# Modulation vectors of the second attention layer: VectorE row products in place of TensorE products on a three-slot weight ring

## The reference

```python
def modulation(cond, w_ada, b_ada):
    m = jax.nn.silu(cond) @ w_ada + b_ada
    return [t[..., None, :] for t in jnp.split(m, 6, axis=-1)]

def modulate(h, shift, scale):
    return h * (1 + scale) + shift
...
    for i in range(DEPTH_2):
...
        sh1, sc1, g1, sh2, sc2, g2 = modulation(c, w_ada[i], b_ada[i])
        csh1, csc1, cg1, csh2, csc2, cg2 = modulation(c_ctx, w_ada[i], b_ada[i])

        h = modulate(rms_norm(x, norm1_g[i]), sh1, sc1)
...
        x = x + g1 * (jnp.concatenate([out_a, out_b, out_c], axis=-1) @ w_out[i])
        x = x + g2 * conv_ffn(modulate(rms_norm(x, norm2_g[i]), sh2, sc2),
                              w_up[i], conv_w[i], conv_b[i], w_down[i])
```

## Time and profile before

| what | value |
|---|---|
| median of 3 runs | 1830.97 us (1829.68 to 1835.06) |
| span of the profiled execution | 1832.5 us |
| own time of the profiled execution | not given beside its span |
| PE busy | 1754.7 us, 96% |
| PE weight loads busy | 1573.7 us, 86% |
| DVE busy | 1031.8 us, 56% |
| ACT busy | 863.4 us, 47% |
| POOL busy | 358.7 us, 20% |
| moved by DMA | 258.76 MB, mean 141 GB/s |

### The profile page before, as it was taken

How to read it: one execution, slowest core, us unless ns; L and a number is a source line. 1 busy time by engine, 2 the same in 40 slices (tenths; PEclk the granted TensorE clock), 3 DMA queues, 4 the chain that set the end, 5 groups by cost and what they waited for, 6 DMA issues and landing times.

```text
span 1832.5 us, 30035 instructions
## 1 busy us (share of the span) xinstructions
PE 1754.7 (96%) x12614; PEld 1573.7 (86%) x12614; DVE 1031.8 (56%) x1804; ACT 863.4 (47%) x1292; POOL 358.7 (20%) x220
## 2 busy tenths in 40 slices
PE   6999989999999999999999999999999898899999
PEld 6999878898999999998867878777888787699999
DVE  2477469687676885267754175413552278538840
ACT  4432546447445665445754254313332355546653
POOL 5301540000000115700001301232114200041147
PEclk9999989999999999999989999999999899889999
DMA  6644445444465554421100422154223222025544
GB/s 262 230 185 163 183 158 205 189 181 178 194 259 205 190 186 143 169 99 47 70 1 12 163 81 98 70 194 177 92 83 126 85 92 75 19 102 198 184 150 150
DMA packets 40967, 258.76 MB, mean 141 GB/s; under 512 B 4352, under 2 KB 7552, under 8 KB 14464
## 3 DMA queue, kind: packets, MB, share of 16 engines
q1 hardware_dynamic: 40832, 256.84, 38.2%
HBM read 255.77 MB, written 1.05 MB: 140 GB/s over the span
## 4 chain that ended last, share of the span: by engine, by line
PE 87%; DVE 9%; ACT 3%; issue 1%; POOL 1%; DMA 0%; SPq 0%; DVEq 0%; ACTq 0%
PE acc_psum L194 24%; PE acc_psum L196 23%; PE acc_psum L195 23%; PE acc_psum L2254 3%; PE acc_psum L235 2%; PE acc_psum L2207 2%; PE acc_psum L319 2%; PE acc_psum L2233 2%; PE acc_psum L923 2%; DVE w_low_sb L160 1%; PE acc_psum L254 1%; DVE norm_rt_sb L1575 1%; POOL w_low_sb L160 1%; DVE norm_sq_sb L579 1%; PE acc_psum L353 0%
## 5 line engine op out<-in xcount | busy, mean ns | idle before, releaser
L194 PE MATMUL acc_psum<-h_high_sb,w_high_sb 128*128 128x256 f32 (+1 forms) x2144 | 666.3, 311 | 10.4 <-DVE h_low_sb L386 4.4
L196 PE MATMUL acc_psum<-h_high_sb,w_low_sb 128*128 128x256 f32 (+1 forms) x2144 | 657.5, 307 | 0.0
L195 PE MATMUL acc_psum<-h_low_sb,w_high_sb 128*128 128x256 f32 (+1 forms) x2144 | 657.4, 307 | 0.0
L149 ACT ACTIVATE w_high_sb<-ring_sb 128x1024 fp32r<-128x1024 f32 (+2 forms) x412 | 386.6, 987 | 455.9 <-PE acc_psum L196 262.1
L194 PEld LDWEIGHTS acc_psum<-h_high_sb,w_high_sb 128*128 128x128 f32 x2144 | 411.0, 192 | 41.6 <-issue 18.2
L160 POOL TENSOR_TENSOR w_low_sb<-ring_sb,w_high_sb 128x1024 fp32r<-128x1024 f32 (+2 forms) x150 | 297.6, 2008 | 687.9 <-ACT w_high_sb L149 687.9
L195 PEld LDWEIGHTS acc_psum<-h_low_sb,w_high_sb 128*128 128x128 f32 x2144 | 410.8, 192 | 19.3 <-issue 0.5
L196 PEld LDWEIGHTS acc_psum<-h_high_sb,w_low_sb 128*128 128x128 f32 x2144 | 410.1, 191 | 19.0
L160 DVE TENSOR_TENSOR w_low_sb<-ring_sb,w_high_sb 128x1024 fp32r<-128x1024 f32 (+1 forms) x262 | 306.5, 1211 | 54.8 <-ACT w_high_sb L149 45.4
L1796 DVE SCALAR_TENSOR_TENSOR u_filtered<-acc_psum,par_sb,u_filtered 128x255 f32<-128x255 f32 (+2 forms) x264 | 150.9, 572 | 151.3 <-ACT u_filtered L1903 139.1
L1931 POOL TENSOR_TENSOR u_low<-u_filtered,u_high 128x256 fp32r<-128x256 f32 (+1 forms) x66 | 61.0, 925 | 779.6 <-ACT u_high L1924 779.6
(11 more groups left out here) (296 smaller groups left out, 2043.4 us busy)
## 6 DMA issues: line engine op xcount, KB each, us to landing
ring_sb<-in_w_in SPq DMA_DIRECT2D x68, 1024.0 KB, 6.4
ring_sb<-in_w_up SPq DMA_DIRECT2D x66, 1024.0 KB, 4.8
ring_sb<-in_w_ada SPq DMA_DIRECT2D x48, 1024.0 KB, 4.8
ring_sb<-in_w_down SPq DMA_DIRECT2D x48, 704.0 KB, 4.1
ring_sb<-in_w_out SPq DMA_DIRECT2D x12, 1024.0 KB, 5.1
ring_sb<-in_w_br_hg SPq DMA_DIRECT2D x4, 1024.0 KB, 6.9
ring_sb<-in_w_br_ml SPq DMA_DIRECT2D x4, 1024.0 KB, 7.0
ring_sb<-in_w_br_mb SPq DMA_DIRECT2D x4, 1024.0 KB, 8.0
```

The lines of the kernel that those rows point to most:

```text
L149: self.nc.scalar.activation(self.high[:, g % 2, piece], self.ring[:, c % RING, piece], ACT.Copy)\
L194: nc.tensor.matmul(out, sh, mh, start=start, stop=False)
L195: nc.tensor.matmul(out, sh, ml, start=False, stop=False)
L196: return nc.tensor.matmul(out, sl, mh, start=False, stop=stop)
```

## The change

The 24 units of layer 1's `w_ada` leave the hybrid block and PE. They are laid out by rows of the transposed matrix: a unit is 128 x 2 rows of 1024, so that partition p holds two whole rows. Both condition vectors are laid out whole in each partition (`cond_rows`, 1 MB), loaded at the beginning of `out_projection`, and passed through Silu by ACT. For each unit DVE multiplies each of the two rows by each of the two vectors and sums along the row in the same instruction, with the bias as the start of the sum: four instructions, which write the result's column straight away. The products themselves are not used: two go to `mod_products`, two into the ring's slot. The units ride in attention layer 0 alone: behind units 1 to 3 of the output projection, 4, 6 and 8 of the first `up`, all eight of the first `down`, 2, 4, 6 and 8 of the second `up`, and 0 to 5 of the second `down`. The gains of layer 1's norms are computed behind unit 6 of the second `down` instead of unit 1.

```diff
+ROW_RIDES = {"out": (1, 2, 3), "up0": (4, 6, 8), "down0": tuple(range(DT)), "up1": (2, 4, 6, 8), "down1": tuple(range(6))}
...
+class RowModulation:
...
+    def dot(self, dve, n, c):
+
+        core, slot = self.core, self.core.ring[:, c % RING, :].rearrange("p (j k) -> p j k", j=2)
+        core.wait_loaded(dve, c)
+        if n == 0:
+
+            dve.wait_ge(*self.rows_ready.at(1))
+        else:
+
+            dve.wait_ge(self.multiplied.handle, n)
+        for s in range(2):
+            for j in range(2):
+                t, row = 2 * n + j, slot[:, j, :]
+                ins = core.nc.vector.tensor_tensor_reduce(row if s else self.products[:, j, :], row, self.rows[:, s, :], 1.0,
+                                                          self.bias[:, t, 0:1], ALU.mult, ALU.add, self.result[:, t, s:s + 1])
+        ins.then_inc(*self.multiplied.one())
...
@@ out_projection, SP
+            if side:
+
+                for handle, value in first_use[0]:
+                    sp.wait_ge(handle, value)
+                sp.dma_start(side.rows[:, :, :].rearrange("p a b -> p (a b)"), a["cond_rows"]).then_inc(*side.rows_in.dma())
             core.release(sp, g0 + units, side)
@@ out_projection, PE
-                if side:
-                    if n >= 1:
-                        side.reduce(pe, n - 1, m0 + n - 1)
-                    side.multiply(pe, n, core.place(g0 + n) + 1)
                 behind.pe(pe, n)
             behind.pe(pe, units)
-            if side:
-                side.reduce(pe, units - 1, m0 + units - 1)
             norm.spread(pe)
@@ out_projection, ACT
                 core.split_high(act, g0 + n + 1)
+                if side and n == 0:
+
+                    act.wait_ge(side.rows_in.handle, 16)
+                    core.nc.scalar.activation(side.rows[:, :, :], side.rows[:, :, :], ACT.Silu).then_inc(*side.rows_ready.one())
                 behind.act(act, n)
@@ out_projection, DVE
-                if side:
-                    side.copy(dve, n)
+                if n in rides:
+                    side.dot(dve, m0 + rides.index(n), core.place(g0 + n) + 1)
             norm.reciprocal(dve)
-            if side:
-                side.read(dve, units, m0, units)
@@ down, PE
-                if n in rides:
-                    if rides.index(n) >= 1:
-                        side.reduce(pe, rides.index(n) - 1, m0 + rides.index(n) - 1)
-                    side.multiply(pe, rides.index(n), core.place(g0 + n) + 1)
@@ down, DVE
                     residual(t, bank(t)).then_inc(*free.one())
                 if n in rides:
-                    side.copy(dve, rides.index(n))
+                    side.dot(dve, m0 + rides.index(n), core.place(g0 + n) + 1)
@@ AttentionAhead, DVE
+        if n == (1 if self.i == 0 else 6):
             gains = core.mod_gains
+            if self.rows:
+
+                dve.wait_ge(*self.rows.multiplied.at(6))
```

More of the change, by code:

```diff
@@ L81 @@
 BANKS = 3
+RIDES = tuple(range(1, 2 * (N_ADA * P // UNIT), 2))
+ROW_RIDES = {"out": (1, 2, 3), "up0": (4, 6, 8), "down0": tuple(range(DT)), "up1": (2, 4, 6, 8), "down1": tuple(range(6))}
+assert sum(len(v) for v in ROW_RIDES.values()) == N_ADA * P // UNIT
 class Core:
@@ L679, in modulation_slot @@
             layer = 0 if counts[0] < NM else 1
-            stream.append((a["w_ada_2"][NM * layer + counts[layer]], None))
+            stream.append(((a["w_ada_2"], a["w_ada_rows"])[layer][counts[layer]], None))
             counts[layer] += 1
@@ L704, in build @@
                 for half in range(2):
[L705 to L706 removed]
+                    add("w_up_2", range(up0 + FFH * half, up0 + FFH * (half + 1)), "dve", "pool", ROW_RIDES[f"up{half}"])
+                    add("w_down_2", range(down0 + half, down0 + 2 * DT, 2), "pool", "dve", ROW_RIDES[f"down{half}"])
             else:
@@ L775, in residual @@
                     return f
-                side = None if last else mods[1]
+                side = None if last else rows
                 with arena(f"arena_attention{i}"):
@@ L780, in build @@
                                              [written.at(n) for n in (-3, -2)])
[L781 to L784, removed]
-                out_projection(core, H, T, *joined, residual(2), norm2, core.eps[:, 0:1], side)
@@ L875, in conv_at @@
         return sum(1 for i in range(n) if PLACES[i][0] in ("ml_qk", "xbc"))
-    rides = list(range(1, UNITS, 2))
     NM = N_ADA * P // UNIT
-    first_read = sig("mod_first_read")
     GROUPS, GW = 4, W8 // 4
@@ L1481, in _ @@
             act.wait_ge(par_ready.handle, 16)
-            nc.scalar.activation(mods[0].cond[:, :, 0:2], pv("cond", DT), ACT.Silu).then_inc(*cond_ready.one())
+            nc.scalar.activation(mod.cond[:, :, 0:2], pv("cond", DT), ACT.Silu).then_inc(*cond_ready.one())
             for n in range(UNITS + 1):
@@ L1639, in _ @@
                 if n == 2 * NM + 1:
-                    mods[0].read(dve, NM, 0, NM).then_inc(*first_read.one())
+                    mod.read(dve, NM, 0, NM)
                 if n == 4:
@@ L1692, in _, with out_projection @@
             norm2.reciprocal(dve)
-            mods[1].read(dve, len(rides), 0, len(rides) - NM)
     core.taken = UNITS
-    mods[0].taken, mods[1].taken = NM, len(rides) - NM
-def out_projection(core, H, T, operand, order, banks, first_use, residual, norm, eps, side):
+def out_projection(core, a, H, T, operand, order, banks, first_use, residual, norm, eps, side):
     nc, units = core.nc, 4
@@ L1704, in out_projection @@
     core.taken += units
-    m0 = 0
+    rides = ROW_RIDES["out"] if side else ()
     if side:
         m0 = side.taken
-        side.taken += units
+        side.taken += len(rides)
     behind = NormBehind(norm, free, {n: n for n in range(units)})
@@ L1805, in feed_forward @@
             down(core, (uh, ul), T, seg == 1, down_banks, first_use, residual, hooks[p], side,
-                 () if not side else (1, 3) if p else tuple(range(DT)))
+                 ROW_RIDES[f"down{p}"] if side else ())
             written = core.sig("proj_bank_free")
@@ L1810, in feed_forward, with up @@
             done_before = core.sig("proj_acc_ready")
-def up(core, H, T, first, n_units, lead_tap, conv3, tmp, uh, ul, norm, banks, first_use, done_before):
+def up(core, H, T, first, n_units, lead_tap, conv3, tmp, uh, ul, norm, banks, first_use, done_before, side=None, rides=()):
     nc, psum = core.nc, core.psum
+    if side:
+        m0 = side.taken
+        side.taken += len(rides)
     acc, free = core.sig("up_acc_ready"), core.sig("up_bank_free")
```

85 lines of the change are left out of this document (47 added, 38 removed).

## The result

The changed kernel takes 1860.75 us (median of 4 runs, 1857.5 to 1864.58) beside 1832.58 us for the kernel before in the same sitting (1829.68 to 1835.06): a ratio of 1.015, 95% interval 1.0129 to 1.0171. It is 28.2 us slower, where the prediction had 28. In the two profiled executions, 1855.7 against 1832.5, the difference is 23.2 us.

A forecast was written before the change was run, and what follows sets the result against it. PE, busy 96% of the span, was taken as the bound. Hybrid block -13.4, `down` +13.8 and +11.2, output projection +1.3 gave +12.9; with 15 for port and clock, +28: 1830.97 + 28 = 1859 us, range 1836 to 1884.

The forecast's parts named there:

- The rides taken away, -30.5 us: Units of w_ada leaving PE: 13.4 us in the hybrid block's tail, 3.7 output projection, 10.7 first `down`, 2.7 second.
- The dot, 5.5 us: On DVE, one unit's four reductions, each with an accumulator read: 5.5 us, lower end 4.9, upper 6.8.
- The rival of a reduction at half rate: On DVE, each reduction's main part takes 2.44 us, the dot 4.9 us longer: 1898 us, chance 0.05.
- Release at E + 6.4, ready at E + 13.5: In `down`, E ends a unit's last matmul; ring slot released 6.4 us later, unit after next ready at 13.5.
- The sign I had named: In the first `down`, w_down's transfers issued 6 us or more behind the end of a unit's last matmul.
- The stalls: PE waits 5.75 us at units 2, 4, 6 of `down` (4.07 at two in the second), 7.2 at next `up`.
- Port and clock, 15 us: In `down`, DVE and POOL waiting for each other plus a lower granted clock behind gaps: 15 us together.
- the rival in which port and clock cost little: In `down`, the ring binds but port and clock cost little: 1836 or 1844 us, chance 0.16.
- The output projection, +1.3: In layer 0's output projection, 3.7 us gained; late last dot costs 4 us, ACT's late split 1.0: +1.3 us.
- The `up` halves at nothing: In both `up` halves, seven dots cost nothing, covered by DVE's 5.0 us idle in a unit of 11.2 us.
- the one in which the hybrid block's tail gives nothing: In the hybrid block's tail, something beside PE takes over at once: 13 us more, 1872 us, chance 0.06.
- The one in which nothing waits: All 30.5 us of rides less 1.8 in the output projection come back as gain: 1802 us, chance 0.06.

## Why the prediction was right

Its mechanism was the one that decided, and its sum held. That the medians differ by 28.2 us where 28 was forecast is luck: the interval alone allows 24 to 31 us, and the steps below miss by several us on either side and cancel in part. By its own steps:

- *The rides taken away, -30.5 us.* In the hybrid block -12.8 against -13.4. Elsewhere they were worth more than summed. The kernel without rides has 47.6 us from the first residual of the output projection to the norm's spread, against 54.4 before: 6.8 us, where I had summed 3.7 up to the end of the last unit. About 1.7 of the 6.8 (an estimate, 3.4 us at half speed) is clock: the kernel before has a stretch at 0.51 there, and the one without rides runs the same unit at 1.00. Some 0.9 lies behind the last unit, where the reciprocal now comes 4.7 us after E instead of 5.6. Over both `down` and the second `up`, 247.8 against 263.5: 15.7 us for ten, not 13.4. A ride there cost PE about 1.57 us, since the units beside it were longer too (their steps of 9.1 us before less 7.56 now), where I had counted its own 1.34. The stretch at 0.51 in the output projection before:

```profile
1034.30:1037.70 3.40, 3.40 (x10) 2.65 (x9) 0.00 (x0) 0.78 (x1) 0.00 (x0) 0.51 1.00 422
```

- *The dot, 5.5 us.* It was 4.8 to 4.9: four reductions 1.205 us apart, the accumulator's read inside that time. My lower end, 4.9, was nearer; the read added 0.01 us in the chain. The rival of a reduction at half rate is out by this. The Trainium skill's rule (Vector Engine (DVE) Microarchitecture Reference, Points that are easy to get wrong) names another instruction form, `S2S2D2_STT`; taken over to this one it would give 2.4 us for each reduction from two float32 sources in SBUF, an estimate, twice 1.22. The trace shows that it can't be taken over to the reduction used here.
- *Release at E + 6.4, ready at E + 13.5.* Release came at E + 5.86, but the way from there to PE took 8.0 us instead of 7.1, since POOL's first half took 2.72 with an odd dot beside it. E + 13.9: two errors that nearly cancel. The sign I had named, an issue 6 us or more behind E, was met only about: the even units' dots were followed by theirs at E + 5.8 to 6.1.
- *The stalls.* 5.75 us for units 2, 4, 6 and 7.2 for the next `up`. Measured 6.3, 5.2, 5.2 and 6.9, with 1.3 more for an odd unit; together 18.1 + 6.9 + 11.7 = 36.7 us against 17.25 + 7.2 + 13.9 = 38.3. In the second `down` the third stall, 4.07 in my sum, was 0.4 us. The unit ahead of it took 13.7 us, six of them at a granted clock of 0.50, and gave the late unit time to get ready; the sum had no such case.
- *Port and clock, 15 us, a choice between 0 and 27.* Against the kernel without rides PE is busy 7.5 + 9.2 = 16.7 us longer with the same matmuls of the two `down`, which is the clock, and the first unit of the next `up` adds to it (3.8 us at 0.50). So the rival in which port and clock cost little is out, though I had no row that fixed the 15. Clock and stalls don't simply add up, as the second `down` shows, and how much a steady clock would give back stays open. The port's own share was seen in rows and not tried alone.
- *The output projection, +1.3.* Measured -1.2. By the kernel without rides the removal gave 6.8, clock included, and the addition cost 5.6 (53.2 less 47.6), where I had 3.7 and 5.0. POOL did fall beside the last dot: its first reduction took 3.37 us in the chain of waits, 2.1 more than 1.28, and the norm's reciprocal began at E + 7.9 (E = 1026.77) instead of E + 5.6.

```profile
1027.67 3.37 DVE mod_products L292
...
1034.67 0.10 DVE norm_tokens_sb L375
```

That POOL and DVE hold each other up is what the Trainium skill says (SBUF — State Buffer, Who interferes with whom), and the trace agrees: 1.27 us became 2.81 on DVE, 3.39 became 5.20 on POOL.

- *The `up` halves at nothing.* Right for three and four rides (+0.6 us in the first). The reason I gave, DVE's 5.0 us of idle time, was not enough of a reason: with nine rides the same idle time was there, and a slot's release behind the next unit's subtraction cost 52 us.

Of the other rivals, the one in which the hybrid block's tail gives nothing is out by its -12.8 us. The one in which nothing waits gave 1802 us. The kernel with the dot ahead everywhere and the rides moved comes near it, at 1800; that it is a little less goes with rides that were worth more than I had summed. One sum of the range is off by 1: 1830.97 + 52 is 1883, not 1884, which changes nothing.

## What to carry to other kernels

In a ring, the instruction that releases a slot belongs to the critical path of the unit that takes the slot, whatever its engine's idle time says: write down the loop release, load, split, release, and compare it with the time of the units that it spans. If work of an otherwise idle engine reads a slot, put it ahead of that engine's waits and ahead of what feeds later units; here two such moves of a few lines, with the rides shifted to where the loop is long, turned a loss of 1.5% into a gain of 1.7%. When the loop is open, 24 units of vector work cost no time that could be told from leaving them out.

## What the runs showed of the hardware

A multiply with accumulation over 128x1024 float32 from SBUF takes 1.205 us from start to start, the accumulator's read (0.08 us in its row) included. Where such a reduction met a POOL subtraction it took 2.81 us, and POOL's pair 5.20 us instead of 3.39. Matmuls put into TensorE's gaps raised the granted clock from 0.87 to 0.96 in one stage and from 0.89 to 0.92 in the other, and gave no time: the work got 6.1 us shorter, the waits and the added matmuls 10.7 us longer. And the same 212 us of attention took 216 at a lower mean clock in seven of twelve traces, in one kernel from one execution to another.
